# Hybrid decoder step on eight cores: inputs and first weights in one GpSimd queue, a third stream on the first five weight units, and norm squares added on VectorE

## The reference, cut to what matters

```python
x = x + 0.5 * rms(swiglu1(rms(x)))
h = rms(x); a_b, a_c, a_x, b_x, b_gate, g_a, g_b = split(h @ w_in)
y_a = (a_b * conv3(a_c * a_x)) @ w_out_a
y_b = (gelu(b_gate) * rglru(conv4(b_x))) @ w_out_b
x = x + rms((sigmoid(g_a) * y_a + sigmoid(g_b) * y_b) @ w_o)
x = x + 0.5 * rms(swiglu2(rms(x)))
```

## Time and profile before

| what | us |
|---|---|
| median of 3 runs | 1630.02 |
| lowest run | 1625.49 |
| the profiled execution | 1635.43 |
| its span on the slowest core (core 4) | 1633.9 |
| TensorE busy in it | 1543.0 |
| VectorE, ScalarE busy | 769.9, 763.3 |

### The profile page before, as it was taken

One profiled execution on the slowest core, in us unless ns is written; L12 is line 12 of the kernel. 1 busy time (PEld: TensorE's weight loads), 2 busy tenths in 40 slices (PEclk: granted clock), 3 DMA queues, 4 the chain that ended last, 5 costly groups with the idle time before them and its releaser, 6 DMA issues.

```text
span 1633.9 us, 25639 instructions; the slowest of 8 cores (1617.1 to 1633.9 us)
## 1 busy us (share of the span) xinstructions
PE 1543.0 (94%) x8695; PEld 844.7 (52%) x8695; DVE 769.9 (47%) x1445; ACT 763.3 (47%) x1359; POOL 128.0 (8%) x245
## 2 busy tenths in 40 slices
PE   1999999999999899999999699999999999999995
PEld 0555555555555455555555354555555555555553
DVE  1212158756678445622116152127656888523513
ACT  2322347867768546411144223236656687315312
POOL 0000000001000000000000010111110100101100
PEclk9999999999999999999999899999999999999998
DMA  9688784667847885586666765555565544555662
GB/s 186 180 194 205 170 208 142 173 182 156 222 135 195 207 206 160 151 199 146 168 189 186 178 217 194 181 194 189 184 226 181 207 181 155 217 183 175 187 208 79
DMA packets 52480, 297.92 MB, mean 182 GB/s; under 512 B 5248, under 2 KB 12544, under 8 KB 26752
## 3 DMA queue, kind: packets, MB, share of 16 engines
q0 software_dynamic: 34704, 222.84, 50.8%
q1 hardware_dynamic: 17648, 73.43, 13.0%
HBM read 287.90 MB, written 64.45 MB: 216 GB/s over the span
## 4 chain that ended last, share of the span: by engine, by line
PE 80%; DMA 14%; DVE 3%; issue 1%; ACT 1%; SPq 0%; DVEq 0%; ACTq 0%; POOLq 0%
PE P L569 80%; DMA wring<-wall 6%; DMA xs<-xin 4%; DMA wring<-wsc 2%; DMA yout<-xs 1%; DVE fp L587 1%; DVE xs L587 1%; DVE fp L601 1%; ACT fp L583 1%; DVE fp L606 0%; ACT L583 0%; SPq L658 0%; DVE big L587 0%; ACT qp L583 0%; DVEq L934 0%
## 5 line engine op out<-in xcount | busy, mean ns | idle before, releaser
L569 PE MATMUL P<-hy,wring 128*128 128x418 bf16 (+5 forms) x6080 | 1101.0, 339 | 28.1 <-DMA wring<-wsc 13.9
L569 PEld LDWEIGHTS P<-hy,wring 128*128 128x128 bf16 x6080 | 590.5, 97 | 514.4 <-issue 43.3
L583 ACT ACTIVATE fp<-P 128x414 f32<-128x414 f32 (+4 forms) x530 | 267.4, 515 | 647.8 <-PE P L569 629.8
L569 PE MATMUL P<-big,wring 128*128 128x414 bf16 (+3 forms) x2400 | 436.3, 338 | 2.9 <-DVE big L587 1.1
L569 PEld LDWEIGHTS P<-big,wring 128*128 128x128 bf16 x2400 | 233.0, 97 | 192.9 <-issue 5.4
L587 DVE TENSOR_TENSOR big<-P,fp 128x414 bf16<-128x414 f32 (+3 forms) x260 | 149.6, 587 | 372.9 <-PE P L569 327.4
L637 POOL DMA_DIRECT2D wring<-wsc x180 | 95.2, 529 | 966.5 <-PE P L569 964.2
L587 DVE TENSOR_TENSOR fp<-fp 128x414 f32<-128x414 f32 (+4 forms) x138 | 77.7, 565 | 191.8 <-ACT fp L583 186.2
L583 ACT ACTIVATE fp<-fp 128x414 f32<-128x414 f32 (+2 forms) x230 | 120.9, 546 | 21.4 <-DVE fp L601 11.6
L583 ACT ACT_TABLE_LOAD x77 | 98.8, 1283 | 19.6 <-PE P L569 14.9
L583 ACT ACTIVATE qp<-xs 128x414 bf16<-128x414 f32 (+3 forms) x120 | 62.7, 544 | 88.0 <-DMA xs<-xin 66.5
(11 more groups left out here) (37 smaller groups left out, 350.1 us busy)
## 6 DMA issues: line engine op xcount, KB each, us to landing
wring<-wsc POOLq DMA_DIRECT2D x120, 1024.0 KB, 5.8
wring<-wall POOLq DMA_DIRECT2D x40, 1024.0 KB, 12.1
wsc<-wring SPq DMA_DIRECT2D x40, 1024.0 KB, 10.8
wring<-wsc POOLq DMA_DIRECT2D x48, 704.0 KB, 4.7
wring<-wall POOLq DMA_DIRECT2D x16, 704.0 KB, 9.4
wsc<-wring SPq DMA_DIRECT2D x16, 704.0 KB, 7.9
wring<-wsc POOLq DMA_DIRECT2D x12, 512.0 KB, 5.0
xs<-xin SPq DMA_DIRECT2D x4, 828.0 KB, 12.1
```

The costliest lines, as they stand in the source:

```text
L569: ins = e.matmul(o, ev(lhs_list[k]), ev(rhs_list[k]), start=(start and k == 0), stop=(stop and k == nk - 1))
L583: return S.op("act", lambda e: e.activation(out=ev(out), in_=ev(in_), func=func, **kw), reads, writes, dur, tbl=TBL.get(func), prio=prio)
```

## The change

The two order tables, the class offsets and the lag of the second stream (now a table with an entry for each unit) are replaced. The scheduler's model of transfers becomes two queues that share the DMA engines. Beside that:

- x of s0, s1 and s2 and the first weight units go into GpSimd's queue, in a fixed order; SyncE keeps the writes to `wsc`, all stores, and x of s3 and s4.
- s2 (group 1) computes its units 0 to 4 from group 0's ring slots; its own loads from `wsc` begin with unit 5.
- `xs` buffers and `yout` are laid out without gaps, so each piece of x is one run for each partition, and the stores of s0 carry its 16 meta columns along (they are cut off on the host).
- In `pre_norm`, outside the first norms of s0 and s1, the eight squares are added on VectorE in float32 and one product with `ones` follows. In the last `evac` of s4 the last chunk's square is summed by TensorE instead of VectorE.
- The first two units of s0 are cut into eight pieces, one for each chunk of the normed input.

```diff
-LAGB = 47.0
+JOIN = 5
+HEAD = 4
+X2_AFTER = 1
+RG_AFTER = 12
...
-DMA_BW = 330e3
-DMA_LAT = 2.0
+CAST_BW = 265e3
+COPY_BW = 400e3
+DMA_CAP = 0.95
+HW_SHARE = 0.17
+DMA_LAT = 2.4
...
-        def load_x(st, after):
-            base = st.c0 * KC
+        def load_x(st, eng, after):
             step = 2 if st.i == 0 else 4
             for k0 in range(0, KC, step):
-                src = xin[:, base + k0 * st.n:base + (k0 + step) * st.n].rearrange("p (k t) -> p k t", k=step)
-                dst = XS[st.s][:, k0:k0 + step, 0:st.n]
-                S.dma("sp", lambda e, dst=dst, src=src: e.dma_start(out=dst, in_=src), after,
+                src = xin[:, st.c0 * KC + k0 * st.n:st.c0 * KC + (k0 + step) * st.n]
+                dst = XS[st.s][:, k0 * st.n:(k0 + step) * st.n]
+                S.dma(eng, lambda e, dst=dst, src=src: e.dma_start(out=dst, in_=src), after,
                       [R_xs(st, k) for k in range(k0, k0 + step)], step * st.n * 512)
...
         def store_x(st, k0, k1):
-            base = st.out0 * KC
-            dst = yout[:, base + k0 * st.m:base + k1 * st.m].rearrange("p (k t) -> p k t", k=k1 - k0)
-            src = XS[st.s][:, k0:k1, st.o:st.n]
+            dst = yout[:, st.c0 * KC + k0 * st.n:st.c0 * KC + k1 * st.n]
+            src = XS[st.s][:, k0 * st.n:k1 * st.n]
...
+            if st.i <= 1 and gvi == 0:
...
+            else:
+                acc = newf()
+                act(acc[0:m], xs_view(st, 0, o, n), AF.Square, m, [R_xs(st, 0)], [acc])
+                for kc in range(1, KC):
+                    sq = newf()
+                    act(sq[0:m], xs_view(st, kc, o, n), AF.Square, m, [R_xs(st, kc)], [sq])
+                    dst = acc if kc < KC - 1 else newq()
+                    tt(dst[0:m], acc[0:m], sq[0:m], ALU.add, m, [acc, sq], [dst])
+                mm_group(ps[0:m], m, [ones[:, :]], [dst[0:m]], [dst, "ones"], [ps])
...
-                ns = 4 if hc == 0 else 1
+                ns = 8 if st.i == 0 and o == 0 and hc < 2 else 4 if hc == 0 else 1
...
+        def begin(g):
+            for i in GROUPS[g]:
+                if g == 1:
+                    at(g, 0, "load", STREAMS[i], load_x, STREAMS[i], "pool", [("wl", 0, X2_AFTER)])
+                elif g > 1:
+                    at(g, 0, "load", STREAMS[i], load_x, STREAMS[i], "sp", [])
+                at(g, 0, "first", STREAMS[i], pre_norm, STREAMS[i], 0, 0, False)
+
+        first_u = [first(-999.0, load_x, STREAMS[0], "pool", []), first(-998.0, issue_unit, 0, 0),
+                first(-997.0, load_x, STREAMS[1], "pool", [])]
+        head = [first_u[1]] + [first(-997.0 + u, issue_unit, 0, u) for u in range(1, HEAD)]
+        shared = []
         for g, members in enumerate(GROUPS):
...
+            for u in range(JOIN if g == 1 else 0, NUNITS):
+                w = head[u] if g == 0 and u < HEAD else at(g, u, "weights", None, issue_unit, g, u)
+                if g == 0 and u == X2_AFTER:
+                    begin(1)
...
+                if g == 0 and u < JOIN:
+                    shared.append((u, w))
+                if g == 0 and u >= X2_AFTER:
+                    for uu, ww in shared:
+                        for i in GROUPS[1]:
+                            work(STREAMS[i], 1, uu, ww)
+                    shared = []
```

More of the change, by code:

```diff
@@ L154, in _nominal @@
     return list(zip(STARTS[g], ENDS[g]))
-CLASSES = {"first": (0, -74.3),
-           "load": (0, 39.5),
-           "out": (0, -20.9),
-           "post": (1, -11.9),
-           "pre": (1, -178.9),
-           "weights": (0, -249.5),
-           "work": (0, 1.9)}
+CLASSES = {"first": (0, -290.3),
+           "load": (0, -329.7),
+           "out": (0, -24.5),
+           "post": (1, 26.0),
+           "pre": (1, -323.1),
+           "weights": (0, 259.2),
+           "work": (0, 24.3)}
 def _fm(w, cols):
@@ L237 @@
     __slots__ = ("idx", "eng", "fn", "deps", "dur", "kind", "semkey", "tbl", "issue", "users", "nwait",
-                 "ready", "start", "end", "pos", "count", "prio", "key", "allocs", "tiles", "nbytes", "need", "tag")
+                 "ready", "start", "end", "pos", "count", "prio", "key", "allocs", "tiles", "xfer", "need", "tag")
     def __init__(self, idx, eng, fn, deps, dur, kind, prio):
@@ L313, in dma @@
         o.tag = self.tag
-        o.nbytes = nbytes
+        o.xfer = nbytes / (CAST_BW if cast else COPY_BW)
         o.issue = 0.6 if eng == "pool" else 0.1
@@ L331, in finalize @@
             o.nwait = len(o.need)
+            o.end = None
             o.ready = 0.0
@@ L354, in slot_for @@
                     continue
+                if any(ops[a].end is None for a in old.acc):
+                    continue
                 t = 0.0
@@ L361, in slot_for, with dma_rates, dma_advance, release @@
             return best
+        def dma_rates():
+            busy = [q for q in queues if queues[q]]
+            if len(busy) == 2:
+                return {"pool": DMA_CAP * (1 - HW_SHARE), "sp": DMA_CAP * HW_SHARE}
+            return {q: 1.0 for q in busy}
+        def dma_advance(t):
+            for q, r in dma_rates().items():
+                queues[q][0][1] -= (t - dma_now) * r
+            return t
+        def release(o):
+            for u in o.users:
+                uo = ops[u]
+                uo.nwait -= 1
+                t = o.end + (SYNC_LAT if (uo.eng != o.eng or o.kind == "d") else SAME_LAT)
+                if uo.eng == "pe":
+                    t = o.end if o.eng == "pe" else t + PE_MARGIN
+                if t > uo.ready:
+                    uo.ready = t
+                if uo.nwait == 0:
+                    ready[uo.eng].append(uo)
         while remaining:
@@ L389, in finalize @@
                     best = pick
+            landing = min(((dma_now + queues[q][0][1] / r, q) for q, r in dma_rates().items()), default=None)
+            if landing is not None and (best is None or landing[0] <= best[0]):
+                dma_now = dma_advance(landing[0])
+                o = queues[landing[1]].pop(0)[0]
+                o.end = dma_now + DMA_LAT
+                release(o)
+                continue
             assert best is not None, "scheduler deadlock"
@@ L401, in finalize @@
             o.start = st
-            if o.kind == "d":
-                t_free[o.eng] = st + o.issue
-                x = max(st + o.issue, dma_free)
-                dma_free = x + o.nbytes / DMA_BW
-                o.end = dma_free + DMA_LAT
-            else:
-                o.end = st + o.dur
-                t_free[o.eng] = o.end
-                if o.eng == "act" and o.tbl is not None:
-                    cur_tbl = (o.tbl & cur_tbl if cur_tbl else None) or o.tbl
             ready[o.eng].remove(o)
@@ L417, in finalize @@
                 v.left -= 1
-            for u in o.users:
-                uo = ops[u]
-                uo.nwait -= 1
-                t = o.end + (SYNC_LAT if (uo.eng != o.eng or o.kind == "d") else SAME_LAT)
-                if uo.eng == "pe":
-                    t = o.end if o.eng == "pe" else t + PE_MARGIN
-                if t > uo.ready:
-                    uo.ready = t
-                if uo.nwait == 0:
-                    ready[uo.eng].append(uo)
+            if o.kind == "d":
+                t_free[o.eng] = st + o.issue
+                t = t_free[o.eng] if landing is None else min(t_free[o.eng], landing[0])
+                if t > dma_now:
+                    dma_now = dma_advance(t)
+                queues[o.eng].append([o, o.xfer])
+            else:
+                o.end = st + o.dur
+                t_free[o.eng] = o.end
+                if o.eng == "act" and o.tbl is not None:
+                    cur_tbl = (o.tbl & cur_tbl if cur_tbl else None) or o.tbl
+                release(o)
+        while any(queues.values()):
+            t, q = min((dma_now + queues[q][0][1] / r, q) for q, r in dma_rates().items())
+            dma_now = dma_advance(t)
+            queues[q].pop(0)[0].end = t + DMA_LAT
         self.makespan = max(o.end for o in ops)
@@ L499, in sb @@
             return ctx.enter_context(nc.sbuf_tensor(name, shape, dt))
-        XS = [sb(f"xs{i}", [128, KC, NM], F32) for i in range(3)]
+        XS = [sb(f"xs{i}", [128, KC * NM], F32) for i in range(3)]
         HY = [sb(f"hy{i}", [128, 16 * HW], BF16) for i in range(3)]
@@ L742, in dn @@
                      [R_hid(k, s) for k in range(HC)] + [w], [pY])
-            return evac(st, pY, m, oc, y32, R_y32, dcol(ghalf, oc), sqs)
+            return evac(st, pY, m, oc, y32, R_y32, dcol(ghalf, oc), sqs, final=(st.last and ghalf == 4))
         def ma(st, j, w):
@@ L852, in at, with first @@
             which, off = CLASSES[cls]
-            S.prio = nominal[g][u][which] + off + (LAGB * st.pos if st is not None else 0.0)
+            S.prio = nominal[g][u][which] + off + (LAGS[u] * st.pos if st is not None else 0.0)
             S.key = (g, u, cls, st.pos if st is not None else 0)
```

(15 more changed lines are left out.)

74 lines of the change are left out of this document (36 added, 38 removed), and 68 rows, old and new, of tables (ENDS, LAGS, STARTS).

## The result

The changed kernel takes 0.9682 of the time of the kernel before, with a 95% interval of 0.9612 to 0.9753: 1578.26 and 1578.77 us.

What follows compares the result with a forecast made beforehand. TensorE's work plus its losses, mainly at start, hand-over and tail, bounds the kernel. Savings 15.8 + 19.7 + 17.8 + 0.6 = 53.9 take 1635.4 to 1581.5 us, stated as a 1577 median; four fifths of cases within 1557 to 1603.

Steps and rivals of the forecast that it cites:

- Sums on TensorE, −15.8: Pre-norm sums: 90 fewer matmuls with `ones` at 0.1761 us each, taken whole as 15.8 us saved, at least 12.
- 91 additions at nothing: Norms on VectorE: 91 more additions, 51.4 us of work, covered by other streams' products and so costing 0.
- The third rival: Norm chains come out from under their cover, each 4.5 us longer; fully open costs 59 us, giving 1636; chance 0.04.
- The Trainium skill's rule, 0 by the row: Moved x loads: GpSimd issues might wait for VectorE, about 5 us together; profile row showed no held issues, so 0.
- The start, −19.7: Up to 120 us: s0's x alone in front lands at about 10; loss 20.5 instead of 40.2 us.
- The first rival: Up to 240 us: DMA engines set the pace, weights come late, early gain given back; 1597 us; chance 0.08.
- Sharing at nothing: s2's units 0 to 4: five fewer loads from scratch, of 180, are hidden work, so 0 gained.
- The middle, no change ±8: From 120 to 880 us: 20.8 us lost before; new order's effect unknown, so no change, ±8.
- the fourth rival: From 120 to 880 us: the new order also closes half of the 20.8 us lost; 1567 us; chance 0.06.
- The hand-over, −17.8: s0 to s3 near 900 us: store 8, load 10, 183 products as cover; 5 lost instead of 22.8 us.
- The second rival: Near 900 us: s3's loads stay slow behind stores, 17 to 22.8 us still lost; about 1592 us; chance 0.10.
- The tail, −0.6: After the last product: one VectorE addition less in the chain, 0.6 us of 17.6.

## Why the prediction was right

1581.5 was worked out for an execution like the profiled one, and 1578.3 came; the forecast of 1577 for a median holds as well. The gain of 57.2 against 53.9 hides larger errors that cancelled: the start gave 5.1 less, the middle 17.5 that the sum did not hold, and 7.6 went again after 1040. So the terms of TensorE's work and of the hand-over are right by their mechanism, and the closeness of the total is in part luck. By its own terms:

**Sums on TensorE, −15.8: right.** 90 products fewer, and 16.5 for 91 put back.

**91 additions at nothing: right.** Cutting 78 of them short gave no gain. (The prediction counts 8 of them in a norm's chain; there are 7, 4.0 us instead of 4.5.) The two groups that hold them after:

```profile
L631 DVE TENSOR_TENSOR fp<-fp 128x414 f32<-128x414 f32 (+3 forms) x215 | 122.7, 573 | 210.3 <-ACT fp L627 203.0
```

```profile
L631 DVE TENSOR_TENSOR qp<-fp 128x414 bf16<-128x414 f32 (+3 forms) x28 | 16.5, 589 | 8.5 <-ACT fp L627 6.6 <-DVE fp L631 0.7
```

The first grew by 77 instructions and 45.0 us, the second by 13, 7.7 us at 589 ns: 52.7 against the 51.4 worked out. VectorE's busy time grew by 41.0 only, since instructions that overlap count once in it. The third rival (norm chains come out from under their cover) did not happen, but the doubled additions show that it lies near: one more instruction ahead of each costs 18.7.

**The Trainium skill's rule, 0 by the row: right, on a thin test.** GpSimd's issues of x took 2.27 us for s0's four, and 1.07 for s2's two from 25.20 on, while VectorE wrote normed chunks (24.54 to 29.15): 0.54 to 0.57 each, as the casts in the earlier trace rows. The rule of "SBUF — State Buffer" (section "SBUF: two separate sides"), as the prediction applied it, would have shown as held issues; none were held. But only s2's two issues met VectorE at work, and no run shows that the instructions there take both ports, as the rule has it.

**The start, −19.7: mis-sized, 14.6.** Two of its steps nearly held: s0's x in at about 10 (its last square began at 11.78, 4.5 us behind the first; the first product with `hy` stands at 15.74 instead of about 13), and about 5 us open at s2's first norm. From 27.6 to 65 us TensorE did 182 matmuls, so 37.4 − 182 × 0.1761 = 5.3 were lost there, and nothing from 65 to 120. What failed is "up to there TensorE has done about 70 products": up to 27.6 it had done 42 matmuls, and 20.2 were lost instead of 15.5. The chain that ended last shows why:

```profile
5.42 19.15 DMA wring<-wall
24.58 0.14 issue
24.71 0.35 PE P L613
```

The second unit stands in the one queue behind s0's x, the first unit and s1's x: 4368 KB as written between 1.60 and 24.57, 195 GB/s. The prediction's slow bound, every transfer at the 184 GB/s of the earlier trace rows, was nearly the rate that held, and its 29 lost are nearer to the 25.6 than the 20.5 of the sum. And I took the weights behind s1's x as ready when needed. What made the gain is shown in part: by the run with x on SyncE the queue gave 6.1 of the 17.3 us by which s0's x came earlier. That the smaller units gave the rest is read from the timelines alone, since `par` spoils that run beyond s0's x. The first rival (weights that come late up to 240, and all 19.7 gone) came true in these 4.7 us at most; from 27.6 on no wait for `wring<-wall` is left.

**Sharing at nothing: right.** Without it the time is the same.

**The middle, no change ±8: wrong, −17.5.** The loss from 120 to 880 fell from 20.8 to 3.3, more than the fourth rival (half of it) gave. The step that failed is "The new order changes them all and no row shows how; I take no change". The 17.1 us of waits for weights there became 1.7, all from scratch:

```profile
PE P L613 <- DMA wring<-wsc: 1.7, 2, 1.5
```

It is not the layout, the sharing or the number of products in a sum: taking back each of these in the same order, or nearly, left 1 to 7 lost. Nor is it the queue of x, as far as the waits for weights tell: they are 3.1 us with x on SyncE. What is left is the plan: the order tables, the model of transfers and the code for which they were fitted. The new model in the old kernel removed the weight waits and gained nothing; the new tables without the model lose 43 in the changed kernel and 59 in the old. How the 17.5 divide between tables and model stays open, because no kernel here has tables fitted to one without the other.

**After 1040, not foreseen: +7.6.** I had taken this stretch as undisturbed. TensorE now waits there for scratch weights (5.1 us in two waits) and for VectorE's evictions (3.3). All runs with the new tables lose 4.9 or more there, all runs with the old ones at most 1.3, whatever their layout, sums or model: the loss goes with the tables. It isn't the additions: with them cut short it is 7.2. Why the tables lose there stays open.

**The hand-over, −17.8: nearly right, −16.2.** The forecast of 8 for the store and 10 for the load met 10.0 and 11.1. The whole chain to s3's sum was longer than worked out, 931.90 − 891.71 = 40.2 instead of 33.6: 1.2 more to the first store, 3.1 in store and load, 1.3 between the halves and 0.9 at the end. TensorE came late to it too, by 4.4 of waits for scratch weights and by 22 products that took 5.72 instead of 4.05 us behind the longest of them (granted clock 0.72 from 926 to 932), so the two delays lay beside each other and only one was paid. That part is luck. The granted clock there is 0.99 instead of 0.95, and no wait is over 3 us. The second rival (the hand-over stays) fell with both layout runs.

**The tail, −0.6: more, about −1.3.** From the end of the last product with a weight unit to the end of the span it was 17.8 us and is 16.5. One addition is 0.6; TensorE's last wait there also fell, from 1.62 to 0.58 us.

No version beat the changed kernel by more than a measurement tells: without the sharing it is equal, in one run, and simpler.

## What to carry to other kernels

A buffer that is stored, freed and loaded again is a chain, and here a layout with one long run for each partition was worth 11 to 18 us alone, in the old order as in the new. Work moved from an engine busy 95% of the time to one busy half of the time counted in full here; put in the same work once more to see how near the cover's end is. Priorities fitted to a plan are part of that plan: with the tables, the model or the sums changed alone the plan lost some 40 to 85 us in three runs of four, so an undo that re-plans is no clean experiment. Look, too, at what else an edit moves: with x on the other queue a 68 KB load came to stand behind it, and the run no longer measured what it was for.

## What the runs showed of the hardware that I had not expected

A load of 68 KB behind six pieces of x in one queue landed 31.8 us after its issue (4.40 to 36.16) in the run with x on SyncE, and 42.5 in the one with the new tables alone, but 2.0 in the changed kernel, where it stands first. In those two runs the start waited for it and not for s0's x.

In the run with the last chunks on GpSimd, VectorE and GpSimd slowed each other down; the timeline of its end:

```profile
1571.11 0.59 DVE L631 TENSOR_TENSOR fp<-hy,fp 128x414 f32<-128x414 f32 x1 [5.68 <-ACT fp L627]
1571.22 1.40 POOL L635 TENSOR_TENSOR fp<-hy,fp 128x414 f32<-128x414 f32 x1 [19.57 <-ACT fp L627]
1571.81 1.26 DVE L631 TENSOR_TENSOR xs<-xs,fp 128x414 f32<-128x414 f32 x1
1572.76 1.22 POOL L635 TENSOR_TENSOR xs<-xs,fp 128x414 f32<-128x414 f32 x1
1572.99 1.44 DVE L631 TENSOR_TENSOR fp<-hy,fp 128x414 f32<-128x414 f32 x1
```

A VectorE instruction of this kind takes 0.59 us where it comes first and 1.12 to 1.44 in the four that follow beside GpSimd: 2.9 us more for the four, where the two chunks moved to GpSimd would have taken VectorE some 2.4. The Trainium skill says in "SBUF — State Buffer" (section "SBUF: two separate sides") that an instruction of VectorE with two inputs in SBUF and one of GpSimd that reads SBUF hold the shared ports one at a time, each for its whole length. The rows agree with it as far as they go (none shows GpSimd's instruction alone): splitting such work between the two gave nothing.
